# Gathered expert results gated early and added by GpSimd, late products and additions by column halves

## The chip, the cores and the metric

One core of a Trainium2 chip runs the whole program. The metric is the device time of one launch in microseconds (us). Five engines take part: TensorE (PE, matmuls; its weight loads are listed as PEld), VectorE (DVE), ScalarE (ACT), GpSimd (POOL) and SyncE (SP, which here only starts DMAs). Each engine takes its own instructions in order, and the engines meet at semaphores. Everything is in fp32 unless said otherwise.

## The reference

Two layers of a hybrid diffusion step over two groups of tokens: 128 prompt tokens and 256 sample tokens, each a row of 1024 numbers. In each layer and for each group:

```python
h = modulate(rmsnorm(x, norm1_w[l]), sh1, sc1)
x = x + g1 * mixer(h)                  # attention and a state space scan, side by side
h = modulate(rmsnorm(x, norm2_w[l]), sh2, sc2)
x = x + g2 * moe_ffn(h, ...)           # 16 experts, each token goes to two of them
# at the end
y = rmsnorm(x, final_norm_w)
```

moe_ffn computes, for the two chosen experts of a token, silu(h @ w_gate) * (h @ w_up) @ w_down, and sums the two with weights that add up to one. The vectors g1 and g2 (the gates) are rows of 1024 numbers, one for each group.

## The kernel before

Tokens lie on the 128 partitions in NT = 3 tiles (t = 0 is the prompt, t = 1 and 2 are the sample). The tile `x[:, t, :]` (128x1024) is the residual stream. The profile calls `acc`, `xn`, `mixed` and `hT` by the name of the buffer that holds them, `arena`.

**The experts.** The 16 experts are worked through in NB = 10 blocks of 128 rows. For each block: rows of h are gathered by an indirect DMA, turned by TensorE (`rows`, L2320), multiplied with the gate and up weights (`first_half`, L2329, eight steps `kt`), SiLU on ScalarE, product on VectorE (L1659), the product turned back by two transposes (`hid_of`, L2336), copied by VectorE (`copy_hidden`, L1665), multiplied with the down weights (`second_half`, L2344), and the result copied out of PSUM by ScalarE (`store`, L1083). TensorE runs `first_half(b + 1)` ahead of `hid_of(b)`, so that most waits are covered.

**Two kinds of results.** The results of the first seven blocks (`STORED`) go to DRAM. Two indirect DMAs of GpSimd for each tile t (`result`, L804) gather each token's two rows from there: the first into `first_y[t]`, the second into `acc[:, t, :]`. The results of the last three blocks (`LATE = 3`) stay in SBUF and are brought to their tokens by matmuls with weighted selection matrices (`late_product`, L2390): for each tile t, three matmuls j (one for each late block) into each of two banks hf (columns 0 to 511 and 512 to 1023).

**The end of a layer.** For each t, ScalarE scales `acc` (`weighted`, L1094) and VectorE adds the first row with its weight (`weighted`, L1648). For t = 2 alone VectorE then multiplies with the gate g2 and adds to x (`added(2)`, L1653 and L1654). All engines then read how many overflow rounds are needed (`overflow`; here none runs). Then VectorE adds the late sums to `acc` for t = 0 and 1 (`late_added`, L1755), multiplies with the gate (`updated`, L1764) and adds to x (L1765). For t = 2 it multiplies the late sums with the gate (L1757) and adds (L1765). In the program's letters below: W is the weighted sum, G a product with the gate, A an addition to x.

**What follows.** ScalarE takes the sum of squares of x (L870), GpSimd makes of it the inverse root (`norm_rstd`, L712 and L713), and VectorE scales the tile: in layer 0 for the next layer (`normed`, L1204), which TensorE then turns (`norm_transposes`, L1871), in layer 1 for the output (`final`, L1770), which SyncE stores. In layer 0 TensorE's queue has the eight transposes of tile 0 inside the late products of t = 2, after j = 0, and the next layer's first products (L1900) behind the late products. GpSimd's queue holds, in this order: the gathers of results, the check for overflow, `norm_rstd` of the next layer.

The order on every engine is that of the program text. VectorE's helper `step` makes it wait for its own last instruction.

Of the kernel before, what the change touches and what calls it, by code (L numbers as in the profile page):

```python
# [15 lines left out]
DEPTH = 2  # L16
NT = 3
# [74 lines left out]
NB = len(BLOCKS)  # L92
# [99 lines left out]
def hybrid_step(nc, x_prompt, x_sample, cache_k, cache_v, state_ssm, c, c_ctx, norm1_w, norm2_w,  # L192
# [9 lines left out]
    with ctx:  # L202
# [3 lines left out]
        def sem(name):  # L206
            return ctx.enter_context(nc.semaphore(name))
# [162 lines left out]
        s_zero, s_ctxs, s_order = sem("borders_zeroed"), sem("ctx_state_copied"), sem("expert_order_made")  # L370
# [31 lines left out]
        s_w1, s_fin, s_xa = (sem(n) for n in ("second_weighted", "moe_gated", "moe_added"))  # L402
        o_gated = sem("over_gated")
        s_iota, s_sel, s_pos, s_oh, s_idm, s_idx, s_yidx = (sem(n) for n in (
            "iotas_made", "experts_chosen", "positions_mm", "selections_made", "slot_sums_mm",
            "slot_tokens_made", "result_rows_made"))
# [8 lines left out]
        s_rounds, o_pass, o_step, o_rows, o_add, o_c, o_pos, o_sel, o_c0 = (sem(n) for n in (  # L415
            "rounds_counted", "over_passed", "over_step", "over_rows", "over_added", "over_results", "over_positions", "over_column", "over_ids_copied"))
# [73 lines left out]
        def rounds_of(eng, l):  # L490

            eng.wait_ge(s_rounds, l + 1)
            return eng.value_load(rounds[0:1, l:l + 1], min_val=0, max_val=MORE)
# [22 lines left out]
        def _(sp):  # L516
# [53 lines left out]
            for l in range(DEPTH):  # L570
# [7 lines left out]
                for pair, k in MOE_UNITS:  # L578
                    if (pair, k) == (SPLIT[0], 1):
                        sp.wait_ge(s_order, l + 1)  # L580
# [51 lines left out]
        def _(pool):  # L632
# [82 lines left out]
            for l in range(DEPTH):  # L715
# [13 lines left out]
                if l:  # L729
                    pool.wait_ge(s_fin, NT * l)  # L730
# [95 lines left out]
                pool.wait_ge(s_yidx, l + 1)  # L826
                for b in range(2):
                    pool.wait_ge(y_stored[b], 16 * stores_before(b, STORED) * (l + 1) + 16)
                for t in range(NT):
                    result(first_y[t], y_exp, y_idx[:, 0, t:t + 1], Y_ROWS).then_inc(combined[t], 16)  # L830
                    result(acc[:, t, :], y_exp, y_idx[:, 1, t:t + 1], Y_ROWS).then_inc(combined[t], 16)
                overflow(pool, l, gather_again, stop=gather_results)
# [4 lines left out]
        def _(act):  # L837
# [78 lines left out]
            for l in range(DEPTH):  # L916
# [182 lines left out]
                for e in range(NB):  # L1099
                    if e + 1 < NB:  # L1100
                        silu(e + 1, (e + 1) % 2)
                    if e == NB - 2:
                        act.wait_ge(s_yidx, l + 1)
# [33 lines left out]
        def _(dve):  # L1137
# [80 lines left out]
            for l in range(DEPTH):  # L1218
# [296 lines left out]
                def one_hots(a, b):  # L1515

                    for e in range(a, b):
                        if e > HOTS:
                            dve.wait_ge(s_idm, SLOT_SUMS * l + e - HOTS)
                        for part in stores_of(e):  # L1520
# [16 lines left out]
                                  ).then_inc(s_order, 1)  # L1537
# [34 lines left out]
                def combination():  # L1572
# [32 lines left out]
                    dve.tensor_copy(rounds[:, l:l + 1], R(4)[:, 9:10]).then_inc(s_rounds, 1)  # L1605
                    dve.wait_ge(s_rounds, l + 1)
                    result_rows(step, y_idx, wt, cap_stored)
                    dve.sem_inc(s_yidx, 1)
# [42 lines left out]
                def added(t):  # L1651

                    step(dve.tensor_tensor(acc[:, t, :], acc[:, t, :], gate_at[1][grp(t)], ALU.mult))  # L1653
                    step(dve.tensor_tensor(x[:, t, :], x[:, t, :], acc[:, t, :], ALU.add))  # L1654
# [33 lines left out]
                weighted(0)  # L1688
                weighted(1)
                weighted(2)  # L1690
                added(2)
# [33 lines left out]
                def add_results(k):  # L1725
# [8 lines left out]
                    assert n[0] == RESULT_STEPS  # L1734
                    dve.sem_inc(o_rows, 1)
# [12 lines left out]
                def late_added(t):  # L1748

                    dve.wait_ge(s_add, NT * l + t + 1)  # L1750
                    for hf in range(2):
                        cols = slice(hf * 512, (hf + 1) * 512)
                        late = bank[ADD_BANK[t][hf]][:, :]
                        if t < 2:
                            ins = dve.tensor_tensor(acc[:, t, cols], late, acc[:, t, cols], ALU.add)  # L1755
                        else:
                            ins = dve.tensor_tensor(acc[:, t, cols], late, gate_at[1][grp(t)][:, cols], ALU.mult)  # L1757
                    ins.then_inc(s_fin, 1)

                def updated(t):  # L1760

                    dve.wait_ge(s_fin, NT * l + t + 1)
                    if t < 2:
                        step(dve.tensor_tensor(acc[:, t, :], acc[:, t, :], gate_at[1][grp(t)], ALU.mult))  # L1764
                    dve.tensor_tensor(x[:, t, :], x[:, t, :], acc[:, t, :], ALU.add).then_inc(s_xa, 1)  # L1765
# [11 lines left out]
                updated(0)  # L1777
                if l == DEPTH - 1:
                    late_added(1)
                    updated(1)  # L1780
                    final(0)
                    late_added(2)
                    updated(2)
                    final(1)
                    final(2)
                else:
# [3 lines left out]
                    updated(1)  # L1790
                    late_added(2)
                    updated(2)
# [6 lines left out]
        def _(pe):  # L1799
# [94 lines left out]
            for l in range(DEPTH):  # L1894
# [588 lines left out]
```

## Time and profile before

| what | us |
|---|---|
| median of 3 runs | 777.38 (775.66, 777.38, 777.53) |
| the profiled execution, whole | 776.23 |
| its span | 774.5 |
| TensorE busy | 724.9 (94%) |
| VectorE busy | 324.9 (42%) |
| ScalarE busy | 213.1 (28%) |
| GpSimd busy | 138.2 (18%) |

The span runs from the first to the last instruction; 1.7 us of the execution lie around it. The end of layer 0 lies at 363 to 406 us of the span, that of layer 1 at 728 to 774.5. A line of the timeline gives the start, the duration, the engine, the line of the program, the operation, output and input, shape and count; in square brackets the engine's idle time before it and what ended it. Instructions of one line that follow on each other are merged. A 128x512 fp32 matmul shows as two of the instructions counted, 0.43 us apart, while the clock is full.

### The profile page before, as it was taken

How to read it: one execution, taken by the hardware profiler on the slowest of the kernel's cores; microseconds unless marked ns; L12 is line 12 of the kernel's file. 1: busy time of each engine (PE TensorE's matmuls, PEld its weight loads, DVE VectorE, ACT ScalarE, POOL GpSimd, SP SyncE). 2: the span in 40 equal slices, each digit the busy share in tenths (PEclk: the TensorE clock that was granted, in tenths of full speed). 3: DMA queues.
4: the chain of work that ended last, by engine and by line, in shares of the span. 5: the costliest groups of instructions: out<-in, count | busy, mean ns of one | idle time of the engine just before them, and what ended most of it. 6: DMA issues, size and time to landing. Idle time of an engine off the chain costs nothing.

```text
span 774.5 us, 10382 instructions
## 1 busy us (share of the span) xinstructions
PE 724.9 (94%) x3940; PEld 354.9 (46%) x3940; DVE 324.9 (42%) x877; ACT 213.1 (28%) x486; POOL 138.2 (18%) x232
## 2 busy tenths in 40 slices
PE   3999998999999999998999999889999899999994
PEld 1447553446445534433344755334544653443331
DVE  2022625637635553312362252473763555231137
ACT  2220145845024101011212024574502310110131
POOL 4056032220010101101112503322001011010202
PEclk9999999999999999999999999999999999999998
DMA  8997335989309899999896233578720389999962
GB/s 319 387 355 263 110 115 212 331 315 364 110 3 337 325 382 391 423 421 423 311 388 230 98 108 116 178 258 306 264 110 4 133 324 390 412 422 423 421 246 82
DMA packets 65639, 209.33 MB, mean 270 GB/s; under 512 B 7736, under 2 KB 8608, under 8 KB 53299
## 3 DMA queue, kind: packets, MB, share of 16 engines
q1 hardware_dynamic: 52744, 179.33, 60.2%
q10 hardware_dynamic: 7723, 16.65, 5.7%
q0 software_dynamic: 5120, 12.66, 4.5%
q8 instruction: 32, 0.52, 0.3%
q14 instruction: 20, 0.16, 0.1%
HBM read 199.92 MB, written 12.88 MB: 275 GB/s over the span
## 4 chain that ended last, share of the span: by engine, by line
PE 75%; DMA 9%; DVE 5%; ACT 4%; SPq 3%; issue 2%; POOL 1%; ACTq 1%; POOLq 0%; DVEq 0%
PE bank L2329 14%; PE bank L2213 11%; PE bank L1955 8%; PE bank L2344 7%; PE bank L2012 5%; PE bank L1900 4%; PE bank L1824 4%; DMA arena<-in_w_up_dram 3%; PE bank L1941 3%; SPq L534 2%; PE bank L2390 2%; DMA ring<-in_w_ada_dram 2%; PE bank L2320 2%; PE bank L2057 2%; DMA arena<-y_exp,y_idx 2%
## 5 line engine op out<-in xcount | busy, mean ns | idle before, releaser
L2329 PE MATMUL bank<-ring,work 128*32 128x512 f32 (+1 forms) x640 | 116.0, 597 | 4.4 <-DMA arena<-in_w_up_dram 3.7
L2329 PEld LDWEIGHTS bank<-ring,work 128*32 128x32 f32 (+1 forms) x640 | 33.7, 121 | 78.1 <-issue 75.0
L2344 PE MATMUL bank<-ring,xs_tok 128*64 128x512 f32 (+2 forms) x320 | 65.7, 597 | 1.5 <-DVE xs_tok L1665 1.0
L1665 DVE COPY xs_tok<-bank 128x256 f32<-128x256 f32 x20 | 8.5, 425 | 138.3 <-PE bank L2336 138.3
L1955 PE MATMUL bank<-arena,ring 128*128 128x384 f32 x192 | 62.2, 486 | 0.0
L2329 PE MATMUL bank<-arena,work 128*64 128x512 f32 (+1 forms) x128 | 58.6, 612 | 0.0
L1824 PE MATMUL bank<-ring,cpad 128*32 128x512 f32 x384 | 50.8, 621 | 7.2 <-DMA ring<-in_w_ada_dram 5.7
L797 POOL DMA_INDIRECT gather_at<-h_rows,idx x18 | 18.2, 1011 | 176.6 <-PE bank L2320 121.2
L1955 PEld LDWEIGHTS bank<-arena,ring 128*128 128x128 f32 x192 | 36.5, 190 | 25.0
L1076 ACT ACTIVATE xs_tok<-bank 128x256 f32<-128x256 f32 x20 | 7.7, 384 | 132.0 <-PE bank L2329 132.0
L2213 PE MATMUL bank<-ring,arena 128*128 128x512 f32 x96 | 43.6, 597 | 0.0
L2213 PE MATMUL bank<-ring,xs_tok 128*128 128x512 f32 x96 | 43.2, 592 | 0.0
L1900 PE MATMUL bank<-ring,arena 128*128 128x512 f32 x96 | 42.8, 597 | 0.4 <-ACT arena L887 0.4
L2012 PE MATMUL bank<-ring,arena 128*128 128x512 f32 x96 | 42.3, 593 | 0.0
L1083 ACT ACTIVATE qkv<-bank 128x512 f32<-128x512 f32 x36 | 19.5, 595 | 74.6 <-PE bank L2344 74.6
L2344 PEld LDWEIGHTS bank<-ring,xs_tok 128*64 128x64 f32 (+2 forms) x320 | 20.5, 131 | 35.0 <-issue 31.4
L1548 DVE COPY work<-bank 128x512 f32<-128x512 f32 x38 | 24.6, 687 | 18.2 <-PE bank L2320 14.5
L1256 DVE SCALAR_TENSOR_TENSOR conv<-arena,prm,conv 128x388 f32<-128x388 f32 x48 | 29.9, 623 | 1.7
L1305 DVE CUSTOM_DVE_ANT_0 arena<-bank,amask 128x384 f32<-128x384 f32 (+1 forms) x48 | 20.1, 466 | 23.9 <-PE bank L2029 23.6
L2213 PEld LDWEIGHTS bank<-ring,xs_tok 128*128 128x128 f32 x96 | 18.2, 190 | 23.0 <-issue 23.0
L2329 PEld LDWEIGHTS bank<-arena,work 128*64 128x64 f32 (+1 forms) x128 | 20.6, 166 | 16.7 <-issue 16.7
L1900 PEld LDWEIGHTS bank<-ring,arena 128*128 128x128 f32 x96 | 17.7, 190 | 22.6 <-issue 20.4
(381 smaller groups left out, 1085.6 us busy)
## 6 DMA issues: line engine op xcount, KB each, us to landing
ring<-in_w_ada_dram SPq DMA_DIRECT2D x48, 1024.0 KB
ring<-in_w_down_dram SPq DMA_DIRECT2D x28, 1024.0 KB
ring<-in_w_gate_dram SPq DMA_DIRECT2D x24, 1024.0 KB
ring<-in_w_up_dram SPq DMA_DIRECT2D x24, 1024.0 KB
ring<-in_w_in_dram SPq DMA_DIRECT2D x16, 1024.0 KB
ring<-in_w_out_dram SPq DMA_DIRECT2D x8, 1024.0 KB
arena<-in_w_gate_dram SPq DMA_DIRECT2D x8, 1024.0 KB
arena<-in_w_up_dram SPq DMA_DIRECT2D x8, 1024.0 KB
```

The source lines that it names most:

```text
L1083: act.activation(y_buf(e)[:, hf * 512:(hf + 1) * 512], bank[5 + hf][:, :], ACT.Copy).then_inc(s_yc, 1)
L1256: ins = dve.scalar_tensor_tensor(out=conv[:, m, :], in0=xpd[:, m, k:k + CONVW], scalar=tap(k), in1=conv[:, m, :], op0=ALU.mult, op1=ALU.add)
L1305: dve.tensor_tensor_reduce(out=probs(t, h), in0=bank[SCORE_BANK[i // 2 % 2][i % 2]][:, 0:nk], in1=amask[:, m0:m0 + nk // P, :].rearrange(" ...
L1548: dve.tensor_copy(xgT[:, b, hf * 512:(hf + 1) * 512], bank[3 + hf][:, :]).then_inc(s_xgc, 1)
L1824: last = mm(bank_of(i)[ADA_TILE * q:ADA_TILE * (q + 1), :], cpad[:, c:c + ADA_TILE], slot(ADA_AT[j])[:, kt, :], start=j == a and kt < ADA_ ...
L1900: last = mm(bank[t][:, :], tok(kt, t), slot(u[0])[:, kt, :], start=kt == 0, stop=kt == KT - 1)
L1941: last = mm(bank[3 + t][:, 0:256], tok(kt, t), slot(u[1])[:, kt, 0:256], start=kt == 0, stop=kt == KT - 1)
L1955: last = mm(bank[(6 + m) % 8][:, 0:3 * P], slot(v)[:, kt, col:col + P], hT[:, kt, :], start=kt == 0, stop=kt == KT - 1)
L2012: last = mm(bank[4 + t][:, :], tok(kt, t), slot(u[3])[:, kt, :], start=kt == 0, stop=kt == KT - 1)
L2213: last = mm(bank[2 * t + hf][:, :], mixed[:, t, kt * P:(kt + 1) * P] if kt < 4 else xs_tok[:, t, (kt - 4) * P:(kt - 3) * P], slot(u + hf)[ ...
L2329: last = mm(bank[b][at:at + n, :].rearrange("p (i f) -> p i f", i=2), rows_T[:, kt * P + at:kt * P + at + n], gate_up_of(s)[:, kt, :, :], ...
L2344: last = mm(bank[5 + hf][at:at + n, :], hidT[:, b, f * P + at:f * P + at + n], w[:, f, hf * 512:(hf + 1) * 512], start=f == 0, stop=f == 1)
```

## The change

It does five things, in both layers.

1. VectorE multiplies the gathered results of every t with the gate right behind their weighted sum (`gated_results`). It was done there for t = 2 alone.
2. GpSimd adds these to x, for every t, between the gathers and its check for overflow. VectorE waits for the addition of t (`s_xp`) ahead of the late sums of t.
3. TensorE makes the late products of t = 1 and 2 one half of the columns after the other, and counts each half (`s_add` rises twice for each t).
4. VectorE multiplies the late sums of each half with the gate, straight from PSUM, and adds them to x by halves.
5. `hid_of(8)`, the two transposes of the ninth block, moves into `first_half(9)`, ahead of its step kt = 6. In layer 0 the transposes of tile 0 for the next layer now stand behind one late product of t = 2, where two stood.

```diff
@@ gpsimd
                 for t in range(NT):
                     result(first_y[t], y_exp, y_idx[:, 0, t:t + 1], Y_ROWS).then_inc(combined[t], 16)
                     result(acc[:, t, :], y_exp, y_idx[:, 1, t:t + 1], Y_ROWS).then_inc(combined[t], 16)
+                for t in range(NT):
+                    pool.wait_ge(s_accg, NT * l + t + 1)
+                    pool.tensor_tensor(x[:, t, :], x[:, t, :], acc[:, t, :], ALU.add).then_inc(s_xp, 1)
                 overflow(pool, l, gather_again, stop=gather_results)
@@ vector
-                def added(t):
-
-                    step(dve.tensor_tensor(acc[:, t, :], acc[:, t, :], gate_at[1][grp(t)], ALU.mult))
-                    step(dve.tensor_tensor(x[:, t, :], x[:, t, :], acc[:, t, :], ALU.add))
+                def gated_results(t):
+
+                    dve.tensor_tensor(acc[:, t, :], acc[:, t, :], gate_at[1][grp(t)], ALU.mult).then_inc(s_accg, 1)
...
-                weighted(0)
-                weighted(1)
-                weighted(2)
-                added(2)
+                for t in range(NT):
+                    weighted(t)
+                    gated_results(t)
...
                 def late_added(t):
 
-                    dve.wait_ge(s_add, NT * l + t + 1)
+                    dve.wait_ge(s_xp, NT * l + t + 1)
                     for hf in range(2):
                         cols = slice(hf * 512, (hf + 1) * 512)
-                        late = bank[ADD_BANK[t][hf]][:, :]
-                        if t < 2:
-                            ins = dve.tensor_tensor(acc[:, t, cols], late, acc[:, t, cols], ALU.add)
-                        else:
-                            ins = dve.tensor_tensor(acc[:, t, cols], late, gate_at[1][grp(t)][:, cols], ALU.mult)
-                    ins.then_inc(s_fin, 1)
-
-                def updated(t):
-
-                    dve.wait_ge(s_fin, NT * l + t + 1)
-                    if t < 2:
-                        step(dve.tensor_tensor(acc[:, t, :], acc[:, t, :], gate_at[1][grp(t)], ALU.mult))
-                    dve.tensor_tensor(x[:, t, :], x[:, t, :], acc[:, t, :], ALU.add).then_inc(s_xa, 1)
+                        k = 2 * NT * l + 2 * t + hf + 1
+                        dve.wait_ge(s_add, k)
+                        dve.tensor_tensor(acc[:, t, cols], bank[ADD_BANK[t][hf]][:, :], gate_at[1][grp(t)][:, cols],
+                                          ALU.mult).then_inc(s_fin, 1)
+                        dve.wait_ge(s_fin, k)
+                        ins = dve.tensor_tensor(x[:, t, cols], x[:, t, cols], acc[:, t, cols], ALU.add)
+                    ins.then_inc(s_xa, 1)
@@ tensor
                 def late_results():
 
                     for t in range(NT):
-                        for j in range(LATE):
-                            if t == 0:
+                        order = [(hf, j) for hf in range(2) for j in range(LATE)]
+                        if t == 0:
+                            order.sort(key=lambda v: v[1] == LATE - 1)
+                        for hf, j in order:
+                            if t == 0 and hf == 0:
                                 result_copied(j)
-                            if t == 2 and j == 1 and l + 1 < DEPTH:
+                            if (t, hf, j) == (NT - 1, 0, 1) and l + 1 < DEPTH:
                                 norm_transposes(2 * l + 2, 0)
-                            for hf in range(2):
-                                if (t, j, hf) != (0, 0, 0):
-                                    last = late_product(t, j, hf)
-                        last.then_inc(s_add, 1)
+                            if (t, hf, j) != (0, 0, 0):
+                                last = late_product(t, j, hf)
+                            if j == LATE - 1:
+                                last.then_inc(s_add, 1)
 
                 for b in range(NB):
                     if b + 1 < NB:
-                        first_half(b + 1, None if b else lambda kt: lists(2) if kt == 6 else None)
-                    hid_of(b)
+                        first_half(b + 1, (lambda kt: lists(2) if kt == 6 else None) if b == 0 else
+                                   (lambda kt: hid_of(NB - 2) if kt == 6 else None) if b == NB - 2 else None)
+                    if b != NB - 2:
+                        hid_of(b)
```

The calls of `updated` go, and the overflow code waits for `s_xp` before it touches x. Three semaphores (the order of the experts, the rounds counted, the result rows made) become one that counts to three in each layer.

## Rows read from the trace of the kernel before

**Rows 1.** The page: TensorE's busy time, and the chain that ended last, by engine.
```profile
PE 724.9 (94%) x3940; PEld 354.9 (46%) x3940; DVE 324.9 (42%) x877; ACT 213.1 (28%) x486; POOL 138.2 (18%) x232
PE 75%; DMA 9%; DVE 5%; ACT 4%; SPq 3%; issue 2%; POOL 1%; ACTq 1%; POOLq 0%; DVEq 0%
```
**Rows 2.** Timeline of VectorE, end of layer 0.
```profile
381.09 1.27 DVE L1648 SCALAR_TENSOR_TENSOR arena<-gather_at,wt,arena 128x1024 f32<-128x1024 f32 x1
...
385.25 1.22 DVE L1653 TENSOR_TENSOR arena<-arena,conv 128x1024 f32<-128x1024 f32 x1
...
389.75 1.29 DVE L1755 TENSOR_TENSOR arena<-bank,arena 128x512 f32<-128x512 f32 x2 [2.02 <-PE bank L2390]
...
392.34 1.22 DVE L1765 TENSOR_TENSOR x<-x,arena 128x1024 f32<-128x1024 f32 x1
395.70 0.75 DVE L1204 TENSOR_SCALAR arena<-x,rstd 128x1024 f32<-128x1024 f32 x1 [2.14 <-POOL rstd L713]
```
**Rows 3.** Timeline of TensorE, the same stretch.
```profile
376.69 3.65 PE L2344 MATMUL bank<-ring,xs_tok 128*64 128x512 f32 x16 [0.52 <-DVE xs_tok L1665]
...
394.70 1.88 PE L2390 MATMUL bank<-qkv,conv 128*128 128x512 f32 x4
396.52 1.09 PE L1871 MATMUL bank<-ident,arena 128*128 128x128 f32 x8
```
**Rows 4.** Timeline of GpSimd, the same stretch.
```profile
394.83 0.19 POOL L712 TENSOR_SCALAR ss<-ss 128x1 f32<-128x1 f32 x1 [24.00 <-ACT arena L870]
395.11 0.56 POOL L713 TENSOR_TENSOR rstd<-ss,epst 128x1 f32<-128x1 f32 x1
```
**Rows 5.** Timeline of GpSimd and VectorE in the mixer of layer 1.
```profile
484.68 3.04 POOL L767 TENSOR_TENSOR xs_tok<-xs_tok,vec 128x512 f32<-128x512 f32 x3
...
485.92 0.86 DVE L1282 TENSOR_TENSOR dtw<-dtr,da 128x48 f32<-128x48 f32 x1
```
**Rows 6.** Timeline of GpSimd, end of layer 1.
```profile
761.00 1.24 POOL L712 TENSOR_SCALAR ss<-ss 128x1 f32<-128x1 f32 x1 [23.30 <-ACT arena L870]
762.32 1.55 POOL L713 TENSOR_TENSOR rstd<-ss,epst 128x1 f32<-128x1 f32 x1
```
**Rows 7.** Timeline of VectorE, end of layer 1.
```profile
748.61 1.28 DVE L1648 SCALAR_TENSOR_TENSOR arena<-gather_at,wt,arena 128x1024 f32<-128x1024 f32 x1 [2.56 <-ACT arena L1094]
750.81 1.28 DVE L1648 SCALAR_TENSOR_TENSOR arena<-arena,wt 128x1024 f32<-128x1024 f32 x1 [0.92 <-ACT arena L1094]
...
755.92 1.29 DVE L1755 TENSOR_TENSOR arena<-bank,arena 128x512 f32<-128x512 f32 x2 [1.30 <-issue]
...
758.50 1.23 DVE L1765 TENSOR_TENSOR x<-x,arena 128x1024 f32<-128x1024 f32 x1
...
762.22 1.22 DVE L1765 TENSOR_TENSOR x<-x,arena 128x1024 f32<-128x1024 f32 x1
...
769.77 1.28 DVE L1770 SCALAR_TENSOR_TENSOR arena<-x,rstd,work 128x1024 f32<-128x1024 f32 x1 [0.92 <-POOL rstd L713]
```
**Rows 8.** Groups of GpSimd's instructions by line: busy, mean ns, idle before.
```profile
L762 POOL TENSOR_TENSOR conv<-xs_tok,dt 128x256 f32<-128x256 f32 x12 | 6.9, 609 | 66.9 <-ACT xs_tok L968 66.9
...
L767 POOL TENSOR_TENSOR xs_tok<-xs_tok,vec 128x512 f32<-128x512 f32 x6 | 6.1, 1042 | 0.2
...
L750 POOL TENSOR_TENSOR gather_at<-gather_at,work 128x320 f32<-128x320 f32 x4 | 3.4, 860 | 0.3
```
**Rows 9.** Windows: busy of PE, PEld, DVE, ACT, POOL; PEclk, DMA share, GB/s.
```profile
364.75:367.02 2.27, 0.01 (x2) 0.03 (x1) 0.00 (x0) 1.08 (x2) 1.90 (x2) 1.00 1.01 422
367.47:370.73 3.26, 3.26 (x10) 1.07 (x8) 0.00 (x0) 0.00 (x0) 2.65 (x3) 0.52 1.00 408
```
**Rows 10.** Chain that ended last, in order of time, end of layer 1.
```profile
736.71 12.85 DMA arena<-y_exp,y_idx
```
**Rows 11.** Timeline of TensorE, end of layer 1.
```profile
745.77 3.65 PE L2344 MATMUL bank<-ring,xs_tok 128*64 128x512 f32 x16 [0.50 <-DMA ring<-in_w_down_dram]
...
762.33 1.88 PE L2390 MATMUL bank<-work,qT 128*128 128x512 f32 x4
```

More of the change, by code:

```diff
@@ L369, in hybrid_step @@
         s_pool, s_dve = sem("pool_step"), sem("dve_step")
-        s_zero, s_ctxs, s_order = sem("borders_zeroed"), sem("ctx_state_copied"), sem("expert_order_made")
+        s_zero, s_ctxs, s_plan = sem("borders_zeroed"), sem("ctx_state_copied"), sem("order_rounds_and_result_rows_made")
         s_prmT, s_prm, s_a = sem("prm_transposed"), sem("prm_copied"), sem("a_made")
@@ L401, in hybrid_step @@
         s_add = sem("late_results_mm")
-        s_w1, s_fin, s_xa = (sem(n) for n in ("second_weighted", "moe_gated", "moe_added"))
+        s_w1, s_accg, s_xp, s_fin, s_xa = (sem(n) for n in (
+            "second_weighted", "results_gated", "results_added", "moe_gated", "moe_added"))
         o_gated = sem("over_gated")
-        s_iota, s_sel, s_pos, s_oh, s_idm, s_idx, s_yidx = (sem(n) for n in (
+        s_iota, s_sel, s_pos, s_oh, s_idm, s_idx = (sem(n) for n in (
             "iotas_made", "experts_chosen", "positions_mm", "selections_made", "slot_sums_mm",
-            "slot_tokens_made", "result_rows_made"))
+            "slot_tokens_made"))
         s_bt, s_btc, s_h = sem("h_transposed_back"), sem("h_rows_copied"), sem("h_rows_stored")
@@ L414, in hybrid_step @@
         RESULT_STEPS = 11
-        s_rounds, o_pass, o_step, o_rows, o_add, o_c, o_pos, o_sel, o_c0 = (sem(n) for n in (
-            "rounds_counted", "over_passed", "over_step", "over_rows", "over_added", "over_results", "over_positions", "over_column", "over_ids_copied"))
+        o_pass, o_step, o_rows, o_add, o_c, o_pos, o_sel, o_c0 = (sem(n) for n in (
+            "over_passed", "over_step", "over_rows", "over_added", "over_results", "over_positions", "over_column", "over_ids_copied"))
         o_oh, o_idm, o_idx, o_w, o_g, o_tx, o_xgc, o_gu, o_sil, o_hid, o_th, o_htc, o_dn, o_yc, o_yst = (
@@ L490, in rounds_of @@
         def rounds_of(eng, l):
-            eng.wait_ge(s_rounds, l + 1)
+            eng.wait_ge(s_plan, 3 * l + 2)
             return eng.value_load(rounds[0:1, l:l + 1], min_val=0, max_val=MORE)
@@ L579, in _ @@
                     if (pair, k) == (SPLIT[0], 1):
-                        sp.wait_ge(s_order, l + 1)
+                        sp.wait_ge(s_plan, 3 * l + 1)
                     if k < 2 and RANK_OF[2 * pair + k] is not None:
@@ L729, in _ @@
                 if l:
-                    pool.wait_ge(s_fin, NT * l)
+                    pool.wait_ge(s_fin, 2 * NT * l)
                 for b, w in ((0, 2), (130, 4), (390, 2)):
@@ L824, in gather_results @@
                     pool.wait_ge(o_add, 2 * NT * (k + 1) + 1)
-                pool.wait_ge(s_yidx, l + 1)
+                pool.wait_ge(s_plan, 3 * l + 3)
                 for b in range(2):
@@ L1102, in _ @@
                     if e == NB - 2:
-                        act.wait_ge(s_yidx, l + 1)
+                        act.wait_ge(s_plan, 3 * l + 3)
                         weighted(0)
@@ L1536, in _ @@
                 dve.tensor_scalar(order, R(4)[:, 16 + FIXED:16 + E], -1.0, float(E), ALU.mult, ALU.add
-                                  ).then_inc(s_order, 1)
+                                  ).then_inc(s_plan, 1)
                 one_hots(*LISTS[0])
@@ L1604, in combination @@
                         step(dve.tensor_tensor(R(4)[:, 9:10], R(4)[:, 9:10], R(4)[:, 10:11], ALU.add))
-                    dve.tensor_copy(rounds[:, l:l + 1], R(4)[:, 9:10]).then_inc(s_rounds, 1)
-                    dve.wait_ge(s_rounds, l + 1)
+                    dve.tensor_copy(rounds[:, l:l + 1], R(4)[:, 9:10]).then_inc(s_plan, 1)
+                    dve.wait_ge(s_plan, 3 * l + 2)
                     result_rows(step, y_idx, wt, cap_stored)
-                    dve.sem_inc(s_yidx, 1)
+                    dve.sem_inc(s_plan, 1)
                 def late_weights():
@@ L1734, in add_results @@
                     assert n[0] == RESULT_STEPS
+                    dve.wait_ge(s_xp, NT * (l + 1))
                     dve.sem_inc(o_rows, 1)
@@ L1776, in _ @@
                 late_added(0)
-                updated(0)
                 if l == DEPTH - 1:
                     late_added(1)
-                    updated(1)
                     final(0)
                     late_added(2)
-                    updated(2)
                     final(1)
@@ L1789, in _ @@
                     modulated(k, 0)
-                    updated(1)
                     late_added(2)
-                    updated(2)
                     for t in (1, 2):
```

## The prediction

> **What bounds the kernel now.** I read the page first, then the chain, then the timelines of the two places that the change touches. The page has TensorE busy for 94% of the span and on 75% of the chain that ended last [rows 1]. So a change on another engine matters where TensorE waits for it, and in the last 25 us, where TensorE no longer sets the end. There are two such places.
>
> The end of layer 0. The late products run without a gap, then TensorE turns tile 0 of the next layer at 396.52 [rows 3]. The scaled tile is ready at 395.70 + 0.75 = 396.45 [rows 2], so VectorE and TensorE arrive almost together: TensorE, free at 394.70 + 4 x 0.43 = 396.42, waits 0.1 us. The tile hangs on the addition to x of t = 0, which ends at 392.34 + 1.22 = 393.56 [rows 2]. From there to the scaled tile it takes 2.89 us: the sum of squares 1.27 (393.56 to 394.83), GpSimd 0.84 [rows 4], and the scaling. Ahead of it VectorE had been idle for 2.02 us, waiting for the late products [rows 2]. This idle time is all the slack there is.
>
> The end of layer 1. The last gather lands 12.85 us after its issue at 736.71, at 749.56 [rows 10], and ScalarE's scaling and VectorE's W2 at 750.81 follow on it [rows 7]. From then on VectorE works nearly alone: 1.30 us for the overflow check ahead of 755.92, the addition of t = 0 from 758.50 to 759.73, that of t = 1 from 762.22, and the last output tile at 769.77 to 771.05 [rows 7]. TensorE ends at 762.33 + 1.88 = 764.21 [rows 11].
>
> **How GpSimd and VectorE get on.** GpSimd now adds 128x1024 tiles while VectorE works on SBUF, so this decides. Three readings say that they shut each other out. GpSimd's three 128x512 products start at 484.68, 1.04 us each by their group, spaced by about 1.0; the second ends at about 486.75. VectorE's 128x48 product, with two SBUF inputs, starts at 485.92 and takes 0.86 us, to 486.78 [rows 5, 8]: it is held until GpSimd is through. The other way round, GpSimd's scalar instruction takes 0.19 us alone and 1.24 us at 761.00, to 762.24, and VectorE's next addition starts at 762.22 [rows 4, 6, 7]. The root after it takes 0.56 us alone and 1.55 us at 762.32: it ends at 763.87, 0.43 us after that addition [rows 4, 6, 7]. VectorE's additions were not lengthened there (1.22 us).
>
> "The shared pair is an exclusive lock, not a bandwidth split", says the Trainium skill, SBUF — State Buffer, section SBUF: two separate sides. It names the case: a VectorE instruction with two SBUF inputs against a GpSimd instruction that reads SBUF. The trace agrees (0.86 and 1.24 us), in short instructions alone; by a split, the change would win something, which is the second rival below.
>
> **Size of a GpSimd addition.** The trace has no 128x1024 one. Lower bound: 256 columns take 0.609 us and 512 take 1.042 [rows 8], so 1024 take 1.042 + 2 x 0.433 = 1.91. Upper bound: 320 columns of two full operands take 0.860, times 3.2 is 2.75 [rows 8]. These have the operands of the new instruction, but part of the 0.86 is a fixed cost. With 0.2 us of it fixed (the 0.19 of a one-column instruction [rows 4]) 1024 columns take 0.2 + 0.66 x 3.2 = 2.3. I take 2.3, with 0.05 for the handover.
>
> **Layer 0, step by step.**
> - Moving `hid_of(8)` takes away the 0.52 us for which TensorE waited at 376.69 [rows 3]: the copy of 0.43 us now lies beside the last two kt steps, 1.7 us of matmuls. Everything behind it starts 0.52 earlier, W0 at 380.57 instead of 381.09 [rows 2]. -0.5. If the cover failed, this would be 0.
> - VectorE and GpSimd together now need: three W of 1.32 with their gaps (1.27 and the gap), three G of 1.26, three additions of 2.35 on GpSimd. Since one shuts out the other, these add up, in whatever order: 3.96 + 3.78 + 7.05 = 14.8, from 380.57 to 395.4. Three held instructions have their first 0.14 us done when the lock comes, so 395.0.
> - The overflow check and the first late product with the gate read no second SBUF tile, and hide behind GpSimd's last addition. Then the addition of the first half, the second half's product and addition: 0.60 + 0.67 + 0.68 = 1.95 (halves of rows of 1.29 and 1.22 with their fixed part). Tile 0 of x is done at 396.9, where it was 393.56: +3.3. Three things make the loss: three GpSimd additions (7.05) against one A of VectorE before, two more G in front, and an idle time of only 2.02 us to take them.
> - The scaled tile comes at 396.9 + 2.9 = 399.8. TensorE is there at 396.42 - 0.52 - 0.86 = 395.0, since one product fewer stands ahead. It waits 4.8 us, and then has five products left instead of four: the next layer starts 3.3 + 0.86 = 4.2 us later. Nothing else of GpSimd's queue is late: its check for overflow (about 1.3) ends at 396.3 at the latest, before its first root at 398.2.
> - The clock. Behind the idle 2.27 us at 364.75 the granted clock was 0.52 for 3.26 us, which is the 1.2 GHz level [rows 9]. There 3.26 x 0.48 = 1.6 us were lost. The new gap is twice as long; I add 1.6. At the least this is 0, as the 0.50 us gap at 745.77 [rows 11] brought no drop.
> - The late halves of t = 1 and 2 fill VectorE until 406; tile 1 is needed by TensorE at 410. Hidden, with 3 us of cover.
>
> Layer 0: 4.2 + 1.6 = +5.8 us.
>
> **Layer 1.** Here `hid_of(8)` gives nothing: `second_half(9)` waited for its weights until 745.77 [rows 11], and the gathers are as late as before. W0, G0 and GpSimd's A0 lie in idle time, but A0 (GpSimd's additions are A0 to A2) runs from 746.85 to 749.2, and holds W1 (748.61 before) by 0.6. Then G1 to 751.55, W2 to 752.8, A1 to 755.15, G2 to 756.25, A2 to 758.6, the rest of tile 0 to 760.5, where it was 759.73: +0.8. Behind it the change pays: tile 1 needs four half instructions, 2.8 us, instead of 3.76. Tile 1 is done at 763.3 (763.44 before), the first output at 764.5, tile 2 at 767.2, the second output at 768.5, tile 2's root at 769.3, the last output at 770.6 instead of 771.05. Layer 1: -0.45.
>
> **Sum.** 5.8 - 0.45 = +5.3 us. On the profiled execution's 776.23 this gives 781.6, on the median 777.38 it gives 782.7. The execution lies 1.15 below the median, and the three runs reach from 775.66 to 777.53; I take the middle, a base of 776.8 and **782.1 us**.
>
> **The rivals.**
> - *No clock drop behind the new gap* (a lock as above): +3.7, 780.5. For it: the drop is seen once only. Against it: the gap is twice the 2.27 us that brought one [rows 9].
> - *A half shared port, or short additions.* If both engines go on at a reduced pace, the overlap costs about half: tile 0 comes at 393.7, layer 0 +1.0, layer 1 -1.0, 776.8. With the lock but additions of 1.91 us and no drop, layer 0 is +2.9, layer 1 -0.9: 778.8. For it: one long VectorE instruction against a long GpSimd one isn't among the rows. Against it: the 128x48 product was held for nearly three quarters of a microsecond, to GpSimd's end [rows 5].
> - *GpSimd really works beside VectorE: faster.* Place: both layer ends. In layer 0, VectorE would need 7.7 us for the three W and G, to 388.3, and 2.8 for tile 0, to 391.2; the tile is scaled at 394.1, before TensorE comes at 395.0. TensorE gains the 0.52 and the 0.1 us: -0.6. In layer 1, G2 ends at 753.75, tile 0 at 757.85, tile 1 at 760.65, tile 2 waits for TensorE's end at 764.2 and is done at 765.6, the last output ends at 769.05: -2.0. Together -2.6, 774.2. It decides as soon as a GpSimd addition leaves VectorE's W and G at 1.28 and 1.22 us. Against it stand rows 5 and 6.
>
> That the addition doesn't leave VectorE at all can be left out: the text gives it to GpSimd's queue.
>
> **Chances.** Lock with the drop 0.42, lock without it 0.20, half shared or short 0.18, side by side 0.20. What a measurement of this kernel can tell from no change is 0.3%, 2.3 us: from 775.0 to 779.7. Faster 0.20, the last rival. Same 0.18, the one before it. Slower 0.62. The likeliest case alone spans 779.9 (additions of 1.91, less 3 x 0.4 in layer 0 and some in layer 1) to 785.0 (2.75: three times 0.45 in layer 0, the same again in layer 1 as tile 0 is late). The range of 8 in 10 reaches down into the fast case's upper half, 775.0, and up to 785.0.
>
> **What would show it.** Right: six GpSimd additions of 128x1024 near 2.3 us; VectorE's G1, G2 and the W behind an addition lasting 1.8 to 3.5 us instead of 1.22 to 1.28; the transposes of tile 0 for layer 1 idle for 4 to 5 us behind VectorE's scaling; a granted clock near 0.5 right behind; the last output 12 us behind A2 (758.6 to 770.6). Wrong: W and G at their old length beside GpSimd's additions; transposes without a wait; a clock of 1.0 behind the gap. The `hid_of(8)` step is right if the 0.52 us wait of the down products is gone in layer 0, and the wait for the weights in layer 1 has grown by as much.

## The result

| | kernel before | changed kernel |
|---|---|---|
| median of 7 runs, us | 777.38 (775.66 to 777.53) | 779.46 (777.69 to 781.43) |
| profiled execution, us | 776.23 | 778.50 |
| its span, us | 774.5 | 776.8 |

The ratio to the kernel before is 1.0035, with a 95% interval of 1.0024 to 1.0047; in a later set it was 1.0042 (1.0026 to 1.0058). The change makes the kernel slower by 2.7 to 3.3 us; the two intervals reach from 1.9 to 4.5. The forecast was 782.1, in a range of 775.0 to 785.0, and a change of +5.3: the sign and the mechanism were right, the size was too large by 2.6 us, about half of it. A few executions in the experiments took over 1000 us; the ratios and what is said below of the mean clock are without them.

The first line of the profile's page, answering to [rows 1], already hints at it. TensorE's 724.9 us haven't changed. VectorE is busy for 7.2 us longer, though two of its additions went to GpSimd, and GpSimd for 13.1 us longer.

```profile
PE 724.9 (93%) x3940; PEld 354.7 (46%) x3940; DVE 332.1 (43%) x881; ACT 213.3 (27%) x486; POOL 151.3 (19%) x238
```

**GpSimd and VectorE shut each other out.** The timelines of the two engines at the end of layer 0 answer to [rows 2, 4] (W is L1652 now, G is L1657, the late product L1758, the late addition L1761, GpSimd's addition L835).

```profile
378.24 1.28 DVE L1652 SCALAR_TENSOR_TENSOR arena<-gather_at,wt,arena 128x1024 f32<-128x1024 f32 x1
379.55 1.22 DVE L1657 TENSOR_TENSOR arena<-arena 128x1024 f32<-128x1024 f32 x1
382.31 2.00 DVE L1652 SCALAR_TENSOR_TENSOR arena<-gather_at,wt,arena 128x1024 f32<-128x1024 f32 x1 [1.53 <-ACT arena L1098]
384.35 1.23 DVE L1657 TENSOR_TENSOR arena<-arena,conv 128x1024 f32<-128x1024 f32 x1
385.49 1.28 DVE L1652 SCALAR_TENSOR_TENSOR arena<-arena,wt 128x1024 f32<-128x1024 f32 x1
386.80 3.25 DVE L1657 TENSOR_TENSOR arena<-arena,conv 128x1024 f32<-128x1024 f32 x1
389.98 0.68 DVE L1758 TENSOR_TENSOR arena<-bank,arena 128x512 f32<-128x512 f32 x1
390.69 2.34 DVE L1761 TENSOR_TENSOR x<-x,arena 128x512 f32<-128x512 f32 x1
392.95 0.68 DVE L1758 TENSOR_TENSOR arena<-bank,arena 128x512 f32<-128x512 f32 x1
393.67 0.69 DVE L1761 TENSOR_TENSOR x<-x,arena 128x512 f32<-128x512 f32 x1
```

```profile
380.87 2.37 POOL L835 TENSOR_TENSOR x<-x,arena 128x1024 f32<-128x1024 f32 x1 [9.66 <-DVE arena L1657]
385.65 3.32 POOL L835 TENSOR_TENSOR x<-x,arena 128x1024 f32<-128x1024 f32 x1 [2.42 <-DVE arena L1657]
390.14 2.35 POOL L835 TENSOR_TENSOR x<-x,arena 128x1024 f32<-128x1024 f32 x1 [1.16 <-DVE arena L1657]
```

Read the two beside each other. The first addition ends at 383.24 and takes 2.37 us though W1 wants in from 382.31: it isn't slowed, so nothing is shared. W1 lasts 2.00 us, to 1.07 behind the addition's end. The second addition is issued at 385.65, while W2 runs to 386.77; it ends at 388.97, 2.20 behind W2. G2, issued at 386.80, lasts 3.25 us, to 390.05. The third holds the first late addition, 0.69 us long by itself, for 2.34. The late product at 389.98 reads PSUM and one SBUF tile; the third addition is issued 0.16 us after it, and both keep their length, 0.68 and 2.35 us. G1 isn't held (1.23 us), as no addition is out while it runs. All of it stands again at the end of layer 1, on GpSimd with 2.35, 3.32 and 2.35 us, on VectorE in these rows, which answer to [rows 7]:

```profile
751.61 1.78 DVE L1652 SCALAR_TENSOR_TENSOR arena<-gather_at,wt,arena 128x1024 f32<-128x1024 f32 x1 [1.74 <-ACT arena L1098]
...
755.88 3.25 DVE L1657 TENSOR_TENSOR arena<-arena,conv 128x1024 f32<-128x1024 f32 x1
...
759.76 2.34 DVE L1761 TENSOR_TENSOR x<-x,arena 128x512 f32<-128x512 f32 x1
...
762.74 0.69 DVE L1761 TENSOR_TENSOR x<-x,arena 128x512 f32<-128x512 f32 x1
...
772.06 1.28 DVE L1767 SCALAR_TENSOR_TENSOR arena<-x,rstd,work 128x1024 f32<-128x1024 f32 x1 [0.93 <-POOL rstd L714]
```

GpSimd's small instructions for the roots, held in [rows 6] for 1.24 and 1.55 us, take 0.19 and 0.57 now:

```profile
764.70 0.19 POOL L713 TENSOR_SCALAR ss<-ss 128x1 f32<-128x1 f32 x1 [3.15 <-ACT arena L874]
764.98 0.57 POOL L714 TENSOR_TENSOR rstd<-ss,epst 128x1 f32<-128x1 f32 x1
```

By then VectorE's instructions alternate between the late product, which doesn't hold them, and a short addition: the 0.19 us at 764.70 lie inside VectorE's late product of 764.68 to 765.36.

**TensorE pays for it at one place.** Its timeline of the changed kernel, answering to [rows 3], and the granted clock behind the gap (columns as in [rows 9]):

```profile
380.16 3.65 PE L2336 MATMUL bank<-ring,xs_tok 128*64 128x512 f32 x16 [1.44 <-DMA ring<-in_w_down_dram]
...
397.31 1.09 PE L1863 MATMUL bank<-ident,arena 128*128 128x128 f32 x8 [3.00 <-DVE arena L1208]
...
404.23 5.31 PE L1892 MATMUL bank<-ring,arena 128*128 128x512 f32 x12
```

```profile
398.24:402.10 3.86, 3.86 (x8) 1.54 (x7) 3.22 (x8) 2.48 (x6) 0.75 (x2) 0.56 1.05 388
402.10:404.20 2.10, 2.10 (x6) 0.94 (x5) 1.07 (x2) 0.00 (x0) 0.00 (x0) 1.00 1.05 386
```

The next layer's first products start at 404.23, where they started at 400.88: +3.35. The last down products of layer 1 start at 748.95, where they started at 745.77 [rows 11]: +3.2. The delay of layer 0 passes through the whole of layer 1. The last output tile starts at 772.06 where it started at 769.77 [rows 7]: +2.3. So layer 1's end gives 0.9 us back.

### The profile page after: what moved, and what is told of

Its sections match the earlier page's. It is cut to its first block, busy times and chain, and to the rows that moved or that the text cites. A ratio compares the mean times of both kernels' runs of the same rounds, so it can differ in the third digit from the quotient of the medians.

```text
span 776.8 us, 10397 instructions
## 1 busy us (share of the span) xinstructions
PE 724.9 (93%) x3940; PEld 354.7 (46%) x3940; DVE 332.1 (43%) x881; ACT 213.3 (27%) x486; POOL 151.3 (19%) x238
## 4 chain that ended last, share of the span: by engine, by line
PE 75%; DMA 10%; DVE 5%; ACT 3%; SPq 3%; issue 2%; ACTq 1%; POOL 0%; POOLq 0%; DVEq 0%
PE bank L2321 14%; PE bank L2205 11%; PE bank L1947 8%; PE bank L2336 7%; DMA ring<-in_w_down_dram 7%; PE bank L2004 5%; PE bank L1892 4%; PE bank L1816 4%; PE bank L1933 3%; SPq L535 2%; DMA ring<-in_w_ada_dram 2%; PE bank L2382 2%; PE bank L2312 2%; PE bank L2049 2%; PE bank L2037 2%
```

## The experiments

Each kernel was timed in five rounds beside the kernel before on one chip; a ratio is to that. There were two sets of four kernels and two pairs; kernels of different sets are compared by these ratios.

**The changed kernel again**, as the base of the second set.

> The changed kernel itself, beside the next three on one chip. Every theory: 779.5 to 780, 0.3 to 0.4% over the kernel before. It is the base of the comparisons of this set.

Measured: 779.66, ratio 1.0042 (1.0026 to 1.0058). Its profile matters for one thing, the clock:

```profile
397.24 1.09 PE L1863 MATMUL bank<-ident,arena 128*128 128x128 f32 x8 [2.78 <-DVE arena L1208]
398.16 1.02 PE L2382 MATMUL bank<-qkv,conv 128*128 128x512 f32 x2
```

Behind a gap of 2.78 us the two instructions took 1.02, at full clock (in the first profile, 1.73). The half clock came 160 us later, in the middle of layer 1's mixer:

```profile
560.00:564.00 4.00, 4.00 (x32) 2.97 (x30) 3.90 (x13) 0.99 (x3) 0.00 (x0) 0.62 0.20 44
```

**The transposes of the ninth block alone.** In the kernel before:

```diff
-                        first_half(b + 1, None if b else lambda kt: lists(2) if kt == 6 else None)
-                    hid_of(b)
+                        first_half(b + 1, (lambda kt: lists(2) if kt == 6 else None) if b == 0 else
+                                   (lambda kt: hid_of(NB - 2) if kt == 6 else None) if b == NB - 2 else None)
+                    if b != NB - 2:
+                        hid_of(b)
```

> The kernel before with part 5's first half alone: the transposes of the ninth block inside first_half(9). Theory: the wait of 0.52 us for VectorE's copy goes, but the next down product then waits for its weights, which land at about 380 us in layer 0 and 745.8 in layer 1 whatever TensorE does. So no change that can be measured: 777.4, at most 0.5 less, and a wait for the down weights in both layers. Rival: the 0.5 us of layer 0 is a real gain and passes to the end (776.9), and it carries the change's missing loss.

Measured: 777.15, ratio 1.0005 (0.9991 to 1.0020). No gain can be measured, and its timeline of TensorE has the wait for the weights that was expected. VectorE's timeline matters further down: W0 starts at 377.80, and there are two idle times.

```profile
380.24 3.65 PE L2344 MATMUL bank<-ring,xs_tok 128*64 128x512 f32 x16 [1.95 <-DMA ring<-in_w_down_dram]
```

```profile
377.80 1.28 DVE L1648 SCALAR_TENSOR_TENSOR arena<-gather_at,wt,arena 128x1024 f32<-128x1024 f32 x1
382.15 1.28 DVE L1648 SCALAR_TENSOR_TENSOR arena<-gather_at,wt,arena 128x1024 f32<-128x1024 f32 x1 [3.07 <-ACT arena L1094]
...
388.80 1.29 DVE L1755 TENSOR_TENSOR arena<-bank,arena 128x512 f32<-128x512 f32 x2 [1.52 <-PE bank L2390]
...
391.38 1.22 DVE L1765 TENSOR_TENSOR x<-x,arena 128x1024 f32<-128x1024 f32 x1
```

**The changed kernel without them** (the same lines the other way round).

> The changed kernel with the ninth block's transposes put back behind first_half(9). Theory: as above, the same time as the changed kernel, 779.5 within 0.5, since the weights' landing sets the last down product. Rival: the move was worth up to 2 us in the changed kernel (TensorE's late products began 1.4 us earlier than before in its trace), and this comes out at 781 to 781.5.

Measured: 780.74, ratio 1.0052 (1.0037 to 1.0068), against 1.0035 and 1.0042 for the changed kernel: the intervals overlap. The time itself lies outside the 0.5 us that the theory allowed, and just short of the rival's 781. The profile shows 0.5 us of it: W0 starts 0.51 later (378.75), and tile 0 is done 0.50 later (394.86 instead of 394.36). In the kernel before, weights and gathers cover the move; in the changed one VectorE's chain runs on from its start, and nothing covers it. My theory held for the first kernel alone.

**VectorE adds the gathered results itself.**

```diff
-                for t in range(NT):
-                    pool.wait_ge(s_accg, NT * l + t + 1)
-                    pool.tensor_tensor(x[:, t, :], x[:, t, :], acc[:, t, :], ALU.add).then_inc(s_xp, 1)
...
                 for t in range(NT):
                     weighted(t)
                     gated_results(t)
+                    results_added(t)
```

> The changed kernel, but VectorE itself adds the gated results to x (nine VectorE instructions for the three tiles, none on GpSimd). Theory of the lock: an addition costs the pair 2.35 us on GpSimd and 1.26 on VectorE, so VectorE gets through sooner with more work of its own: tile 0 of layer 0 is done at 392.7 instead of 394.4, TensorE waits 1.3 instead of 3.0 us and the clock doesn't drop (1.6), -3.3; in layer 1 VectorE is no longer the bound for tile 2, -1.1. In all 775.1, below the kernel before. Rival: VectorE is overloaded in both, GpSimd takes real work off it, and putting three additions of 1.26 back costs about 3.8 us in layer 0: 783.

Measured: 775.60, ratio 0.9983 (0.9969 to 0.9997). In each layer VectorE has three additions of 1.26 us more to do, 3.8 us, and is through with tile 0 sooner:

```profile
387.36 1.22 DVE L1654 TENSOR_TENSOR arena<-arena,conv 128x1024 f32<-128x1024 f32 x1
388.62 1.23 DVE L1658 TENSOR_TENSOR x<-x,arena 128x1024 f32<-128x1024 f32 x1
...
392.23 0.69 DVE L1763 TENSOR_TENSOR x<-x,arena 128x512 f32<-128x512 f32 x1
```

G2 is 1.22 us again instead of 3.25; tile 0 is done at 392.92 (expected 392.7). The edit moves the additions to the other engine, and with them their place in line (VectorE also waits for each G of its own, as it did in the kernel before). That alone takes the loss away. Whether it makes a gain over the kernel before is less sure, and the end of this section comes back to it. One thing was off: TensorE didn't wait at the transposes, as it came to them late. Its last down products took 5.35 us instead of 3.65 behind a 1.81 us wait for weights; here the half clock fell there.

**Half the width on GpSimd.**

```diff
-                    pool.tensor_tensor(x[:, t, :], x[:, t, :], acc[:, t, :], ALU.add).then_inc(s_xp, 1)
+                    pool.tensor_tensor(x[:, t, 0:512], x[:, t, 0:512], acc[:, t, 0:512], ALU.add).then_inc(s_xp, 1)
```

> The changed kernel with GpSimd adding columns 0 to 511 alone; the other half of the gathered results is left out of x. A dose of the lock: GpSimd's instruction is about 1.2 us instead of 2.35. Theory of the lock: three times 1.1 less for VectorE, tile 0 of layer 0 at 391.1, TensorE doesn't wait for the transposes and its clock stays up: -4.6; layer 1 is bound by TensorE's last products and gains 1.1. In all about 773.8, and VectorE's G2 lasts about 2.2 instead of 3.25 us. Rival: the loss comes from the order (products by halves, one product fewer ahead of the transposes): then within 1 us of 779.5.

This kernel leaves the other half of the columns of the gathered results out of x, so its results are wrong; its counts of instructions are those of the changed kernel. Measured: 774.61, ratio 0.9970 (0.9956 to 0.9984). The dose works on VectorE as the lock says:

```profile
386.50 2.17 DVE L1657 TENSOR_TENSOR arena<-arena,conv 128x1024 f32<-128x1024 f32 x1
388.60 0.68 DVE L1758 TENSOR_TENSOR arena<-bank,arena 128x512 f32<-128x512 f32 x1
389.31 1.26 DVE L1761 TENSOR_TENSOR x<-x,arena 128x512 f32<-128x512 f32 x1
```

GpSimd's addition takes 1.27 us, G2 2.17 instead of 3.25, the held late addition 1.26 instead of 2.34: 1.1 less in each, half an addition. Tile 0 is done at 391.90, 2.5 us sooner than in the changed kernel (expected 3.3: the first addition now ends before W1 wants to begin, and holds nothing).

**The gap filled.** Ahead of the transposes of tile 0:

```diff
                             if (t, hf, j) == (NT - 1, 0, 1) and l + 1 < DEPTH:
+                                clock_kept(3, 6)
                                 norm_transposes(2 * l + 2, 0)
```

> The changed kernel with six matmuls of 128x256 into an unused bank ahead of the transposes of tile 0 for layer 1 (in layer 0), some 2.9 us of work in the 3.0 us gap. Theory: the half clock behind the gap costs 1.7 us (ten instructions of the late products took 5.99 us, at full clock 4.29), and with the gap filled it stays at 1.0: -1.7, 777.9 to 778.2. Rival: the clock falls for another reason, or the gap has nothing to do with it: no change, or +0.3 where the fill is too long.

Measured: 777.74, ratio 1.0022 (1.0010 to 1.0035), against 1.0042 for the changed kernel beside it. The ratios are 1.6 us apart, which is what was expected, but their intervals overlap, and its one profile can't tell, since the changed kernel's profile of this set had no drop at this place either. The wait that is left is 0.70 us.

**Two products ahead of the transposes.**

```diff
-                            if (t, hf, j) == (NT - 1, 0, 1) and l + 1 < DEPTH:
+                            if (t, hf, j) == (NT - 1, 0, 2) and l + 1 < DEPTH:
```

> The changed kernel with two late products ahead of the transposes of tile 0 instead of one, as before. Theory: the transposes wait for VectorE anyway, so the second product fills 0.86 us of the gap, and one product fewer stands behind: -0.9, and the shorter gap may save a part of the 1.7 us of half clock: 777.5 to 779. Rival: the position is without effect: the same as the changed kernel.

Measured: 777.69, ratio 1.0027 (1.0010 to 1.0043), by the ratios 1.2 us under the changed kernel beside it, with overlapping intervals. Its transposes started at 397.35 after a wait of 2.19 us, where the changed kernel's started at 397.24 after 2.78: the extra product went into the gap, and one fewer stood behind.

**In the order of need.** No GpSimd additions; in layer 0, W and G and A of each tile are placed so that the late sums of tile 0 don't wait for those of tiles 1 and 2. Against the kernel in which VectorE adds itself:

```diff
                 for t in range(NT):
                     weighted(t)
-                    gated_results(t)
-                    results_added(t)
+                    if t < 2 or l:
+                        gated_results(t)
+                    if t == 0 or l:
+                        results_added(t)
...
+                    results_added(1)
                     normed(k, 0)
-                    late_added(1)
+                    gated_results(2)
+                    results_added(2)
                     modulated(k, 0)
+                    late_added(1)
                     late_added(2)
```

> No GpSimd additions (VectorE adds), and in layer 0 VectorE's work in the order of need: W, G, A of tile 0, W and G of tile 1, W of tile 2, then the late sums of tile 0, and the rest behind. Theory: the late sums of tile 0 begin as soon as TensorE's first half is there, so TensorE never waits for the transposes, with 1 us more of slack than with all nine ahead; layer 1 as there. 775.0 to 775.6. Rival: TensorE already didn't wait for them with nine ahead, so nothing more is won, and the modulation of tile 0, now behind G2 and A2, may be late: 776.

Measured: 774.12, ratio 0.9978 (0.9965 to 0.9990), 0.9 us under the range that was expected. The late sums of tile 0 now wait for TensorE, not the other way round, and the transposes of layer 1's tile 0 start without a wait at 394.23 (396.52 in the kernel before [rows 3], 395.56 in the run with the transposes alone):

```profile
387.86 0.69 DVE L1762 TENSOR_TENSOR arena<-bank,arena 128x512 f32<-128x512 f32 x1 [1.59 <-PE bank L2389]
```

```profile
394.23 1.04 PE L1870 MATMUL bank<-ident,arena 128*128 128x128 f32 x8
```

This profile had no stretch at half clock while TensorE worked, and has the shortest span of all profiles, 771.0.

**The weights' wait filled**, in the order of need, and in the kernel before.

```diff
                         result_copied(0)
                         late_product(0, 0, 0)
+                        clock_kept(0, 3)
```

> The kernel with VectorE's work in the order of need (no GpSimd additions), and three short matmuls into an unused bank while TensorE waits for the last down weights of each layer (1.1 to 2 us in all profiles). Theory: that wait sometimes brings the half clock (the kernel with all nine on VectorE had it: the down products took 5.35 instead of 3.65 us), the fill of 1.5 us hides in the wait: the same profile where there was no drop, and 0 to 1 us less in the mean: 773.5 to 774.2. Rival: the fill is paid where the wait is short: +0.5 us.

> The kernel before with the same three short matmuls ahead of the last down products, and nothing else. Theory: there the wait is nought to 0.5 us, so the fill of 1.5 us isn't covered in layer 0 unless the weights are late: between 0 and +1.5 us, 776 to 778. Rival: the fill keeps the clock and gives the gain of the kernel in the order of need by itself: 774.5 or less; then that gain would be the clock's, not VectorE's.

Measured: 774.45, ratio 0.9964 (0.9950 to 0.9977), just over the expected 774.2, and 776.36, ratio 0.9997 (0.9986 to 1.0009). The fill alone does nothing that can be measured to the kernel before, so the rival, by which the fill would give the gain by itself, is out. Whether it adds to that order was tried once more, side by side:

> The kernel in the order of need once more, beside the filled one on the same chip: 0.997 to 0.999 of the kernel before, in every theory.

> The filled one once more. Theory: the fill takes away some of the half clock stretches and gives 0.5 to 1 us against the one beside it. Rival: the difference seen so far (0.9964 against 0.9978, in different sets) is the spread between sets, and the two are within 0.3 us here.

Measured: 774.41, ratio 0.9977 (0.9964 to 0.9990), and 773.77, ratio 0.9970 (0.9957 to 0.9983). Twice the filled one is ahead, by 0.5 to 1 us (the first time across two sets), and twice the intervals overlap. That it helps stays open. That the order of need beats both kernels doesn't: it was under 1 with its whole interval in all four runs.

**With the clock taken out.** Every execution has its mean granted clock on record, so the half clock need not be guessed from single profiles. Over the executions of one kernel, the time rises by 0.62 us for each 0.001 that the clock is lower (one slope fitted for all kernels). Brought to one clock by this slope, the kernels lie as follows against the kernel before of the same set (the changed kernel in both its sets against that of the later one). These are estimates, good to about 0.3 us, and they take a stretch at half clock to cost the same wherever it falls.

| kernel | mean clock | us against the kernel before, at equal clock |
|---|---|---|
| before, 99 executions | 0.9938 | 0 |
| before, transposes moved | 0.9935 | +0.2 |
| before, weights' wait filled | 0.9935 | +0.2 |
| changed, 12 executions | 0.9926 | +2.1 |
| changed, without the transposes' move | 0.9920 | +3.1 |
| changed, gap filled | 0.9945 | +1.8 |
| changed, two products ahead | 0.9930 | +1.2 |
| VectorE adds itself | 0.9950 | -0.2 |
| half the width on GpSimd (wrong results) | 0.9940 | -1.9 |
| order of need, twice | 0.9942, 0.9940 | -2.1, -1.9 |
| order of need, filled, twice | 0.9945, 0.9954 | -1.7, -1.6 |

So the changed kernel loses about 2.1 us by its delay and about 0.8 by the clock. Filling the gap won back the clock and little else. The transposes' move is worth 1.0 us in the changed kernel, of which its profiles show 0.5. VectorE's own additions win back the 2.1 us, but what put that run under the kernel before is its higher clock. The order of need is ahead at equal clock too, and its fill adds nothing there. No run separates the parts that it shares with the changed kernel, the early gate and the late sums by halves, so what each of them is worth stays open.

## Why the prediction was right in kind and too large

- **The lock: right.** In the timeline, three GpSimd additions and VectorE's two-tile instructions follow on each other, none of them beside another. The half-width run gives the dose, the run with VectorE's own additions the cause. The side-by-side rival (0.20) is out, the half-shared one too. Of the signs, G2 (3.25) and W1 (2.00) came as named, while G1 kept its 1.23 us and the transposes waited 3.0 us instead of 4 to 5. The rival with short additions (1.91 us, no drop) had the time nearest to the measured one, 778.8, and the one without a drop had 780.5; the first is out as a mechanism, since the additions take 2.35 us, so its number would have been luck.
- **A GpSimd addition of 2.3 us: right.** Measured 2.35 (2.37 in layer 0).
- **The chain from W0 to tile 0: right in length, wrong in its start.** Forecast 16.3 us (380.57 to 396.9), measured 16.1 (378.24 to 394.36). But it started 2.3 us sooner than I had it. I took the start from the profile before less the 0.52 us of `hid_of(8)`. That profile had lost 1.6 us at half clock just ahead of it [rows 9], as it happened in that execution, and waited 2.26 us for the up weights; the changed kernel's waited 1.27 and lost nothing. The run with the transposes alone shows the start without that loss: W0 at 377.80.
- **"This idle time is all the slack there is": the step that was mis-sized.** I had 2.02 us of slack, and from it +3.3 for tile 0. The late W0 of that profile had eaten the rest: VectorE was idle for only 0.25 us ahead of W1, in the row below. In the run with the transposes alone it is idle for 3.07 us there and 1.52 ahead of the late sums, 4.6 in all, and most of the first addition fits into the 3.07. That run has tile 0 done at 392.60, so the change costs tile 0 1.8 us, and not 3.3; against the first profile, whose tile 0 was late itself, it is only 0.8.

```profile
382.61 1.28 DVE L1648 SCALAR_TENSOR_TENSOR arena<-gather_at,wt,arena 128x1024 f32<-128x1024 f32 x1 [0.25 <-ACT arena L1094]
```

- **Moving `hid_of(8)`, -0.5: wrong for the kernel before, nearly right for the changed one (0.5 us in the profiles, about 1.0 at equal clock).** I saw the weights' wait in layer 1 [rows 11] and didn't ask where they land in layer 0: at 380. The wait for them took back 1.44 us there. That start and this wait also shortened the gap at the transposes: the scaled tile came 2.5 us sooner than forecast (397.25 for 399.8), but TensorE, held by the weights, only 0.7 sooner (394.3 for 395.0). The gap was 3.0 us instead of 4.8.
- **One product more behind the transposes, +0.86: right.** From the transposes' start to the next layer's first product, 4.36 us became 6.92. Of these 2.56, 0.86 are the product and 1.7 the clock. The run with two ahead takes the 0.86 back out.
- **The clock, +1.6: the step that failed as a difference.** It is there in the profile, at its forecast size. But the profile before had paid one as well, elsewhere, and so had most others: before at 367, changed at 398, the changed one again at 560, the one without the transposes' move at 399. I counted the new one and not the one that was already in the base. As a mean the gap does cost something: the clock is 0.9926 in the changed kernel, 0.9945 with the gap filled, and 0.9938 in the kernel before. The last difference is worth about 0.8 us, half of the term.
- **Layer 1, -0.45: right in sign, small.** Measured -0.9. Tile 0 was late by 0.5 instead of 0.8, and behind it 1.4 us came back where the forecast had 1.25.

Two profiles that both had their half clock far from these places show the change without that accident: the run with the transposes alone, and the changed kernel of the second set. Layer 1's transposes of tile 0 start at 395.56 and at 397.24, +1.68, which is tile 0's delay; the next layer's first product at 399.92 and at 402.46, +2.54, which is that and the one product more; the last output tile at 770.24 and at 772.16, +1.9. The executions at equal clock say +2.1. Of the forecast +5.3, then, 3.7 was delay and measured 2.1, and 1.6 was clock and measured 0.8.

## What to carry over

Before work is moved from VectorE to GpSimd, look at whether GpSimd's instruction and VectorE's beside it both read two SBUF tiles: here such a pair cost its sum. GpSimd's addition is nearly twice VectorE's (2.35 against 1.23 us), so the "helped" engine got slower while its own list got shorter. Leaving the additions to VectorE took the loss away; the gain came with the order, the tile that TensorE waits for first. And a sum that starts from one profiled execution inherits that execution's accidents: look for stretches at half clock in the base before adding one to the change, and compare the mean clock over many executions.

## What the runs showed of the hardware

- GpSimd against VectorE is no slowing of both. The waiting instruction shows as a long one, with no wait beside it: G2 reads 3.25 us and looks busy. Nor does the waiting lists' view name it. Only its 1.22 us elsewhere give it away.
- A VectorE instruction that takes one operand from PSUM isn't held, and doesn't hold GpSimd: issued 0.16 us ahead of a GpSimd addition, it took 0.68 us, 0.52 of them beside it, and the addition kept its 2.35 us.
- GpSimd's second addition waited for W2 and then went ahead of G2, which came 30 ns after W2's end. It was so at the end of both layers: the one that waited got its turn, and VectorE had no precedence.
- The half clock is not a fixed price of a gap. In these profiles gaps of 1.83, 1.95 and 2.78 us were followed by full clock, and gaps of 1.81, 2.19, 2.26, 3.00 and 3.70 us by some 3.5 us at half. Layer 1's mixer, where no listed wait of TensorE is over 1.2 us, had one too in several profiles:

```profile
504.00:508.00 4.00, 4.00 (x18) 1.13 (x22) 0.68 (x4) 4.00 (x15) 1.22 (x2) 0.57 0.15 19
```

This is the filled kernel in the order of need, whose span was 772.7, against 771.0 and 771.3 for the two profiles of this order without such a stretch. One of 3.5 us costs about 1.7 us, and where in an execution it comes, or whether, differs from run to run of one kernel. It is a good part of the 2 to 7 us by which executions of one kernel differ here; what sets it off was not settled.
